# A streaming encoder layer on one core: the input projection by one level of Strassen's scheme

## The reference, cut to what matters

```
h  = rmsnorm(x, g1)
z  = h @ w_in                      # 1024 x 8200: mq mk mv mo | i f | sb sc sx | dq dk dv | gt (3 x 1024)
ya = sigmoid(mo) * rmsnorm(mlstm(mq, mk, mv, i, f))          # 4 heads, recurrence over 5 token chunks
yb = sb * dwconv3(sc * sx)
yc = rmsnorm(diff_attention(dq, dk, dv))                     # prompt (chunk mask) and sample (1024 cached keys)
x  = x + sum_b(sigmoid(gt_b) * (y_b @ w_branch[b])) @ w_out
h2 = rmsnorm(x, g2);  up = dwconv3(h2 @ w_up)                # 1024 x 5632
x  = x + (silu(up[:2816]) * up[2816:]) @ w_down;  y = rmsnorm(x)
```

## Time and profile before

| | |
|---|---|
| median of 3 runs | 1053.42 us (1052.29 to 1055.95) |
| the profiled execution | 1055.69 us, of which the span is 1053.9 us |
| mean granted TensorE clock | 0.986 of 2.4 GHz |
| PE busy | 97% of the span, 8074 matmuls |
| DVE, ACT, POOL busy | 49%, 33%, 17% |
| DMA | 92 MB, 88 GB/s on average |

### The profile page before, as it was taken

One profiled execution on the slowest core, in us unless ns is written; L12 is line 12 of the kernel. 1 busy time (PEld: TensorE's weight loads), 2 busy tenths in 40 slices (PEclk: granted clock), 3 DMA queues, 4 the chain that ended last, 5 costly groups with the idle time before them and its releaser, 6 DMA issues.

```text
span 1053.9 us, 19077 instructions
## 1 busy us (share of the span) xinstructions
PE 1020.5 (97%) x8074; PEld 994.4 (94%) x8074; DVE 519.3 (49%) x782; ACT 348.6 (33%) x616; POOL 180.1 (17%) x357
## 2 busy tenths in 40 slices
PE   5999999979999999999999999999999999999996
PEld 4899899978988999999999999999999999999996
DVE  6543243413344447234325444777777777533332
ACT  5333232423344333222223332333333433222221
POOL 4101223200222122300002120112211212110010
PEclk8999999989999999999999999999999999999998
DMA  6223214371112142131512422223322222332212
GB/s 186 81 81 85 76 51 123 94 224 56 41 41 81 41 121 81 49 99 55 151 49 71 131 81 81 80 81 96 105 81 81 80 81 84 104 94 86 83 56 86
DMA packets 93452, 92.46 MB, mean 88 GB/s; under 512 B 3492, under 2 KB 86329, under 8 KB 93367
## 3 DMA queue, kind: packets, MB, share of 16 engines
q1 hardware_dynamic: 88559, 82.09, 25.4%
q10 hardware_dynamic: 3784, 6.29, 2.0%
q0 software_dynamic: 1024, 2.86, 1.0%
HBM read 86.15 MB, written 5.08 MB: 87 GB/s over the span
## 4 chain that ended last, share of the span: by engine, by line
PE 92%; DVE 3%; DMA 2%; ACT 1%; POOL 1%; issue 0%; ACTq 0%; DVEq 0%
PE D L1319 83%; DMA ck<-in_cache_k 2%; PE X L1500 1%; PE X L1536 1%; DVE hn_x L1040 1%; PE D L1403 1%; PE X L1470 1%; PE X L1505 1%; PE X L1450 0%; PE X L1447 0%; PE X L1448 0%; PE X L1432 0%; DMA x_t<-in_x_prompt 0%; PE X L1519 0%; PE X L1486 0%
## 5 line engine op out<-in xcount | busy, mean ns | idle before, releaser
L1319 PE MATMUL D<-h_h,w_h 128*128 128x272 f32 (+1 forms) x1744 | 365.7, 291 | 6.8 <-DVE h_l L1034 5.0
L1319 PE MATMUL D<-h_h,w_l 128*128 128x272 f32 (+1 forms) x1744 | 362.0, 289 | 0.0
L1319 PE MATMUL D<-h_l,w_h 128*128 128x272 f32 (+1 forms) x1744 | 360.9, 289 | 0.0
L985 DVE TENSOR_TENSOR w_l<-raw,w_h 128x1024 fp32r<-128x1024 f32 (+3 forms) x172 | 196.8, 1145 | 192.9 <-ACT w_h L752 188.1
L1319 PEld LDWEIGHTS D<-h_h,w_h 128*128 128x128 f32 (+1 forms) x1744 | 273.8, 189 | 9.8 <-issue 4.0
L1319 PEld LDWEIGHTS D<-h_l,w_h 128*128 128x128 f32 (+1 forms) x1744 | 274.8, 189 | 0.4
L1319 PEld LDWEIGHTS D<-h_h,w_l 128*128 128x128 f32 (+1 forms) x1744 | 272.6, 189 | 0.4
L752 ACT ACTIVATE w_h<-raw 128x1024 fp32r<-128x1024 f32 (+3 forms) x172 | 162.1, 943 | 105.0 <-PE D L1319 76.8
L953 ACT ACTIVATE acc<-ups,fcw 128x546 f32<-128x546 f32 x44 | 33.1, 753 | 163.9 <-POOL ffn_last L698 163.9
L1319 PE MATMUL D<-g_h,w_h 128*128 128x272 f32 x352 | 73.4, 290 | 1.8 <-ACT w_h L752 1.8
L1319 PE MATMUL D<-g_l,w_h 128*128 128x272 f32 x352 | 72.7, 288 | 0.0
(11 more groups left out here) (317 smaller groups left out, 1109.7 us busy)
## 6 DMA issues: line engine op xcount, KB each, us to landing
raw<-in_w_in SPq DMA_DIRECT2D x32, 1024.0 KB, 5.7
raw<-in_w_up SPq DMA_DIRECT2D x22, 1024.0 KB, 5.0
raw<-in_w_down SPq DMA_DIRECT2D x16, 704.0 KB, 4.5
raw<-in_w_branch SPq DMA_DIRECT2D x6, 1024.0 KB, 5.0
raw<-in_w_out SPq DMA_DIRECT2D x4, 1024.0 KB, 5.1
x_t<-in_x_prompt SPq DMA_DIRECT2D x4, 512.0 KB, 5.7
ck<-in_cache_k ACTq DMA_DIRECT2D x1, 2048.0 KB, 16.0
cv<-in_cache_v ACTq DMA_DIRECT2D x1, 2048.0 KB, 24.3
```

What stands on the lines that cost most here:

```text
L985: v.tensor_tensor(lo, src, hi.bitcast(F32), ALU.subtract).then_inc(S["wl_ready"], 1)
L1319: last = t.matmul(banks(n)[0:w.shape[2], half, 0:HALF], w[:, k, :], x[:, kx, HALF * half:HALF * half + HALF], start=kx == 0 and i == 0, st ...
```

## The change

The 64 blocks of the input projection and its gates, and the narrow one, are made in 33 pairs (32 of two 128-column blocks, and `i` with `f`). A pair is a matrix product of two token halves (272 each), two k halves (4 slices each) and two column blocks, and is done by seven products `p` of 4 slices, three terms and one token half: 12 matmuls each, 84 for a pair, where 2 blocks had 96. The other matmuls of the kernel stay.

- **Left operands.** Seven arrays (A11, A12, A22 and the sums S1 to S4, each 4 slices by 272), high and low parts, are made once at the start by DVE (`scaled`, `sum_left`, `low_left`) and ACT (`high_left`), spread over the first products (`left` units).
- **Right operands.** Three quarters of the weights are used as they are; four sums T4 to T7 of quarters, 512 wide, are made for each pair by DVE (`make_t`). Each of the seven is split by ACT and DVE into high and low parts, 512 wide.
- **Output.** Products 1, 6, 7 and 4 accumulate one after another in one PSUM bank, and ACT copies the bank out after each, 272 wide. Product 2 has a bank, 5 and 3 share one; DVE adds them to what ACT stored (three additions, 272 wide, per pair). Product 6 waits for ACT's copy of 1, 7 for that of 6, 4 for that of 7, and 3 for DVE's addition of 5.
- **What follows a block** now works on stored data: tanh over both blocks of a pair (1088 wide), the convolution's multiply and `sb`'s; the low parts of `ya` and `yb` go from POOL to DVE (1088 wide).
- **Slots.** Split weights come in five slots of 512 for all products of the kernel, split four units ahead; raw weights in four slots of half the size. The transposes `tok` (two of four 128-column tiles and one `tokS` of the sample tiles, per pair) use PSUM bank 1 alone, which product 2 and half of each `pr` use too.
- **Order.** Written anew: the recurrence's stage 2 and the next stage 0 follow product 7 of a pair, stage 1 follows product 3; `rows` 0, 1 and 2 stand among the first pairs; a step of the prompt attention comes after every five units of work (a `p` counts one, a `pr` two), from the second pair of `gt0` on; `sc`, `sx` and `sb` follow branch 0 all together. `cv` is loaded after `ck` 1, no longer beside `ck`.
- **Residual.** The seven arrays take the room of `xT`, so the transposed x is written to DRAM (`x_spill`, 2.2 MB, an ACT-queue DMA) after the first norm and read back before the output projection.

```diff
+NRAW, NSPLIT = 4, 5
+AHEAD = NSPLIT - 1
...
+A11, A12, A22, S1, S2, S3, S4 = range(7)
+LEFT = {1: A11, 2: A12, 3: S4, 4: A22, 5: S1, 6: S2, 7: S3}
+T_SLOT = {5: 0, 6: 1, 7: 2, 4: 3}
+QUARTER = {1: (0, 0), 2: (1, 0), 3: (1, 1)}
+A_PART = {A22: 5, S1: 6, S2: 7, S4: 8, S3: 9}
+LOW_AT = {A11: 4, A12: 4, S2: 5, S1: 6, S3: 7, A22: 8, S4: 9}
...
+    pair_banks = {pairs[0]: (0, 1, 3), pairs[1]: (2, 4, 5), pairs[2]: (6, 7, 3)}
+    pair_banks.update((q, (2 * (i % 2), 1, 3)) for i, q in enumerate(pairs[3:]))
...
+    unit("left", 0)
+    q_if, q_k0, q_k1, q_q0 = pairs[:4]
+    prod(q_if, 1, 2)
+    unit("left", 1)
+    prod(q_k0, 1, 2)
+    unit("left", 2)
+    prod(q_k1, 1, 2)
+    unit("left", 3)
+    prod(q_if, 6, 5)
+    unit("left", 4)
+    prod(q_k0, 6)
+    prod(q_if, 7)
+    unit("left", 5)
+    prod(q_k0, 5, 7)
+    prod(q_if, 4, 3)
+    prod(q_k0, 4, 3)
     unit("lam")
...
+    for u, q in enumerate((("dk", 1), ("dv", 0), ("dq", 0), ("dv", 1))):
+        follow(q, 7, "ml", 2, u)
+        follow(q, 7, "ml", 0, u + 1)
+        follow(q, 3, "ml", 1, u + 1)
+    follow(("dq", 1), 7, "ml", 2, 4)
...
+    for i, q in enumerate(queue):
+        prev, nxt = pairs[i + 2], queue[i + 1] if i + 1 < len(queue) else None
+        gated = prev[0][:2] == "gt"
+        toks = [tok] if prev[0] in ("mk", "mv", "dk", "dv") else []
+        a, other = pair_banks[q][0], 2 - pair_banks[q][0]
+        started = (q, 1) in [x[1] for x in ORDER if x[0] == "p"]
+        if prev == ("gt0", 3):
+            posts(prev, 0)
+            project(prev, 0, (0, 1), (0, 1))
+            project(prev, 1, (2, 3), (0, 1))
+            gated = False
+        if not started:
+            put(q, 1)
+        if gated and not started:
+            put(q, 5)
+            put(q, 6)
+            posts(prev, 0)
+            put(q, 2)
+        elif prev == ("gt0", 3):
+            put(q, 6)
+            put(q, 2)
+            put(q, 5)
+        else:
+            put(q, 2)
+            posts(prev, 0)
+            put(q, 6)
+            put(q, 5)
+            posts(prev, 1)
+        for f in toks:
+            f(prev, 0)
+        put(q, 7)
+        if gated:
+            project(prev, 0, (min(other, 1), max(other, 1)), (0, 1) if other == 0 else (1, 0))
+        elif nxt and not (q[0][:2] == "gt" and q != ("gt0", 0) and q != ("gt1", 0)):
+            put(nxt, 1)
+        for f in toks:
+            f(prev, 1)
+        put(q, 4)
+        for f in toks:
+            f(prev, 2)
+        put(q, 3)
+        if gated:
+            project(prev, 1, (min(a, 1), max(a, 1)), (1, 0) if a == 0 else (0, 1))
+    last = pairs[-1]
+    posts(last, 0)
+    project(last, 0, (0, 1), (0, 1))
+    project(last, 1, (2, 3), (0, 1))
     for j in range(KD):
         add("wo", j)
     unit("norm", 1)
...
...
+            waits_of[n] += {6: [n_of(q, 1)], 7: [n_of(q, 6)], 4: [n_of(q, 7)], 3: [n_of(q, 5)]}.get(w, [])
+            if w in (1, 2, 5):
+                last_user[banks_of[n][0]] = n_of(q, {1: 4, 2: 2, 5: 3}[w])
...
+        u6 = u_of(q, 6) - AHEAD
+        for w, e in ((7, u6 - 2), (6, u6 - 1), (5, u_of(q, 5) - AHEAD - 1), (4, u_of(q, 4) - AHEAD - 1)):
+            T_MAKES.setdefault(-1 if q == q_if else e, []).append((q, w))
...
+        def chain_bank(pair, w):
+            i = pair_banks[pair][{2: 1, 5: 2, 3: 2}.get(w, 0)]
+            return bank(i)[0:H if pair == q_if else P, 0:HALF]
...
+            def make_t(q, w):
+                i = pair_no[q]
+                B11, B12, B21, B22 = (quarter(q, k, blk) for k in range(2) for blk in range(2))
+                x, y, op = {7: (B22, B12, ALU.subtract), 6: (t_view(q, 7), B11, ALU.add), 5: (B12, B11, ALU.subtract),
+                            4: (B21, t_view(q, 6), ALU.subtract)}[w]
+                for k in {7: (0, 1), 6: (0,), 5: (0,), 4: (1,)}[w]:
+                    wait_item(dve, (q, k))
+                if i >= 2:
+                    dve.wait_ge(S["wl_ready"], u_of(pairs[i - 1], w) + 1)
+                if w in (6, 4):
+                    dve.wait_ge(S["t_ready"], t_no[(q, {6: 7, 4: 6}[w])] + 1)
+                v.tensor_tensor(t_view(q, w), x, y, op).then_inc(S["t_ready"], 1)
...
+                            scaled(k, 1, f_21[:, k, :])
+                            scaled(k + KQ, 1, a_f[:, A22, k, :])
+                        dve.wait_ge(S["f_ready"], 16)
+                        sum_left(S1, f_21[:], a_f[:, A22], ALU.add)
+                        dve.wait_ge(S["s_ready"], 1)
+                        sum_left(S2, a_f[:, S1], f_half[:, 0], ALU.subtract)
+                    elif a[0] == 1:
+                        dve.wait_ge(S["s_ready"], 2)
+                        sum_left(S4, f_half[:, 1], a_f[:, S2], ALU.subtract)
+                        dve.wait_ge(S["s_ready"], 3)
+                        low_left(S2)
+                    elif a[0] == 2:
+                        low_left(S1)
+                        sum_left(S3, f_half[:, 0], f_21[:], ALU.subtract)
+                    else:
+                        low_left({3: S3, 4: A22, 5: S4}[a[0]])
                 elif kind == "norm":
...
+                    dve.wait_ge(S["dense_done"], n + 1)
+                    wait_drained(dve, n_of(q, {2: 1, 3: 6}.get(w, 7)))
+                    out, src = dst_of(q, *{2: (0, 0), 3: (1, 0)}.get(w, (1, 1))), chain_bank(q, w if w in (2, 3) else 5)
+                    v.scalar_tensor_tensor(out=out, in0=src, scalar=scale_of(q), in1=out, op0=ALU.mult, op1=ALU.add)\
+                        .then_inc(S["dve_drained"], 1)
...
+                elif kind == "left":
+                    if a[0] == 0:
+                        act.wait_ge(S["f_ready"], 16)
+                        act.dma_start(x_spill, xT0[:]).then_inc(S["x_out"], 16)
+                        high_left(A22, ("f_ready", 16))
+                        high_left(S1, ("s_ready", 1))
...
+                elif kind == "p" and a[1] in (1, 6, 7, 4):
+                    q, w = a
+                    blk, half = {1: (0, 0), 6: (1, 0), 7: (1, 1), 4: (0, 1)}[w]
...
+                    act.dma_start(xT[:], x_spill).then_inc(S["x_back"], 16)
...
+            def strassen_product(n, q, w):
+                g, left = first_unit[n], LEFT[w]
+                pe.wait_ge(S["wl_ready"], g + 1)
+                if q == q_if and w > 2:
+                    pe.wait_ge(S["al_ready"], LOW_AT[left])
+                wh, wl, out = split_view(w_h, g), split_view(w_l, g), chain_bank(q, w)
+                for k in range(KQ):
+                    if q == q_if and w == 1:
+                        pe.wait_ge(S["al_ready"], k + 1)
+                    for i, (wt, x) in enumerate(((wh, a_h), (wh, a_l), (wl, a_h))):
+                        last = t.matmul(out, wt[:, k, :], x[:, left, k, :], start=w in (1, 2, 5) and k == i == 0,
+                                        stop=k == KQ - 1 and i == 2, skip_group_check=True)
+                last.then_inc(S["dense_done"], 1)
...
+                        dve.wait_ge(S["x_back"], 16)
```

1048 lines of the change are left out of this document (601 added, 447 removed), and 3 rows, old and new, of the table ML_ORDER.

## The result

| | before | after |
|---|---|---|
| median of 4 runs | 1053.72 us (1052.29 to 1055.95) | 1107.80 us (1106.51 to 1108.14) |
| ratio | | 1.0509, 95% interval 1.0493 to 1.0524 |
| profiled execution, span | 1053.9 us | 1106.2 us |
| mean granted clock of the span | 0.986 | 0.964 |

The change makes the kernel 5.1% slower. 1062 us were predicted, with 1088 as the upper end: the sign was right, the size was not, and the range missed it by 20 us.

What follows compares the result with a forecast made beforehand. PE was taken to bound the kernel, DVE the `sc` to `sb` stretch. From 1055.7 us, -43.5 for matmuls and added waits sum to +8.5, 1064.2; the median of runs is 2.3 lower: 1062 us, range 1026 to 1088.

Steps and rivals of the forecast that it cites:

- the pauses at `rows`: Among the first pairs, DVE and ACT bursts outlast PE's cover: +12 us taken, bounds 5 and 15.
- `ck`: Load behind the recurrence: the 5.3 us wait grows by up to 1.5; with `sample` and `mo` +4 us, bounds 0 and 7.
- the start: Until PE is in full flow at about 57 us, making the left operands costs +7 us, bounds +4 and +12.
- `sc` to `sb` stretch: Six pairs after branch 0: DVE needs 99.0 us against PE's 81.5, so +19 us, bounds 10 and 24.
- A: Rival for the waits at `rows`, recurrence and `sample`: bursts are absorbed, faster, 1033 us; chance with its far end 0.27.
- D: Rival on the matmul count: the change doesn't save the matmuls, time above 1100 us; chance 0.01.
- B: Rival on DVE: every added instruction costs its full duration, +15 to 20 us, 1079 us; chance with beyond 0.18.
- -43.5 + the waits: Whole kernel: 348 fewer matmuls at 0.125 us save 43.5 us, and added waits are put against that: +8.5 us.
- the recurrence: Four recurrence steps: DVE's stage 1 makes PE wait 1.5 to 1.9 us each, +7 us, bounds 2 and 10.
- the attention beside branch 0: Gate pairs with attention steps: PE 21.3 us against DVE 19.2, PE stays the bound, +1 us, bounds 0 and 5.
- branch 2: Late stretch counted in the rest: DVE stays hidden, +1 us for the change-over, bounds 0 and 3.
- The upper bounds of the waits: All added waits at their largest, about 80 us together, give 1090 us.

Runs made afterwards that it cites:

- its best version: Changed kernel with attention only beside gates, tok transposes in banks 4 and 5, `rows` 1 cut, branch 2's product 2 first, transpose copies on ACT: 1082.76 us, ratio 1.0281.
- after_best: Changed kernel with attention, bank, `rows` 1, product 2 and transpose-copy edits, plus idle matmuls (24 and 48) in two pauses: 1082.44 us, ratio 1.0268.

## Why the prediction was wrong, step by step

**Right: what bounds, the matmuls, most of the waits.** 7726 matmuls; PE's pace of 0.125 at full clock; the pauses at `rows` (3.8, 4.6 and 4.6 us for 2.3, 5.4 and 4.7, the second released by the copy into `mk_tok` that the text named); `ck` 7.2 us for 5.3 + up to 1.5; the start, 4.4 for 7 with the lower bound at 4; 20.6 for 19 in the `sc` to `sb` stretch. That the three pauses at `rows` add up to the forecast is partly luck, since the first was 1.5 us longer and the second 0.8 shorter. No rival took place. The bursts were not absorbed (A). The matmuls were saved (D): its time, above 1100, came true, but the count is 7726 and the pace at full clock 0.125. B's 1079 was too low, and its reason fails too, as DVE's next instruction still starts 0.60 us after a split:

```profile
75.99 0.67 DVE L1226 TENSOR_TENSOR w_l<-tw,w_h 128x512 fp32r<-128x512 f32 x1
76.59 0.42 DVE L1379 SCALAR_TENSOR_TENSOR mkT<-D,mkT 128x272 f32<-128x272 f32 x1
```

**The step that failed: "-43.5 + the waits" as the whole sum.** It priced each wait at its length and took every matmul at 0.125 us. The sum lacked 44 us (1064.2 for 1108.0). 11 of them are waits that were longer or not foreseen (63.2 for 52); the other 32.6 are time in which the matmuls that are left ran slower: 19 us of granted clock, some 12 us at the edges of the interruptions. The clock stood in the text for the start's upper bound alone, although shows what a pause does in mid-kernel: 26 matmuls in six us behind the 5.3 us wait, where the earlier trace rows has 8 in each (though 16 of the 26 are transposes of 128 columns). By its pace a matmul is 0.10 us dearer there. The five long pauses that came (3.8, 4.6, 4.6, 7.2 and 5.45 us, three of them foreseen at about this length) have 6.8 us at the low level each, up to 3 us beyond themselves, and the eight other stretches of 3.4 us 1.5 each. The fills show that the clock is a real cost in this kernel (10.5 us from four pauses), and also that it doesn't always come back as time: two other fills gave nothing that can be told.

**Mis-sized: the recurrence, 10.0 for 7; the attention beside branch 0, 3.2 for 1.** Same mechanism as foreseen, longer chains.

**Missing: branch 2, 7.4 for 1.** The text asked whether PE has enough work beside DVE's and found that it had. It did not follow who frees the place that ACT's copy of product 1 needs. Before, a gate block was copied by a tanh of its own block, 9 us apart; now the copy stands between products 1 and 6.

**Right number, partly wrong reason: `sc` to `sb`.** The text had DVE busy for over 90% of the stretch. It was busy for 83.2 of 111 us, 75%, and PE idle for 16.9:

```profile
375.00:486.00 111.00, 94.11 (x661) 85.04 (x660) 83.16 (x162) 50.29 (x135) 22.53 (x52) 0.95 0.21 58
```

So it is no full engine that holds PE up, but in-order lists that wait for each other by turns: the longest wait, 5.45 us, is for ACT's `y_tmp`, and ACT itself had stood 8.0 us for a sum of DVE's that came behind a convolution:

```profile
438.46 0.79 DVE L1538 SCALAR_TENSOR_TENSOR scb<-u_c,vec,scb 128x546 f32<-128x546 f32 x1
...
439.89 0.68 DVE L1241 TENSOR_TENSOR tw<-tw,raw 128x512 f32<-128x512 f32 x1
...
440.61 0.63 ACT L985 ACTIVATE w_h<-tw 128x512 fp32r<-128x512 f32 x1 [8.02 <-DVE tw L1241]
...
443.50 0.36 ACT L1188 ACTIVATE y_tmp<-X,vec 128x128 f32<-128x128 f32 x1
...
444.01 1.09 PE L1849 MATMUL X<-ident,prob 128*128 128x128 f32 x4 [5.45 <-ACT y_tmp L1188]
```

Taking work from DVE helps (11.6 and 34 us), but a comparison of sums, 99.0 against 81.5, gave the right cost by luck as much as by method.

**The range.** The upper bounds of the waits (about 80 us) gave 1090, and the range ended at 1088. A cost that multiplies the waits belonged to it. By what was measured here it is 0.5 us of slower matmuls for each us of added pause (32.6 by 63.2), which on 80 us is 40 and would have moved the upper end to 1130; the clock alone (0.3) would have moved it to about 1114.

## What to carry to other kernels

A matmul saved on a PE that never waits is worth its pace only if nothing else begins to wait: here 43.5 us of matmuls were paid with 63 us of waits, and the waits with some 19 us of clock and 12 at their edges. When a forecast creates pauses on PE, price the long ones with the slow matmuls that follow one in the profile at hand, not with their length alone. Where such a pause can't be avoided, matmuls that nobody reads can hold the clock; whether the time follows has to be measured: it did in one of three kernels here. And in-order engines that wait for each other lose time long before one of them is full, so cut a burst and look at what stands behind it before comparing sums of busy time.

## What the runs showed of the hardware

- Eight pauses of PE in a dense stretch, in one execution: those of 0.3 to 1.92 us left the granted clock at full; those of 2.35, 2.64 and 2.93 us were each followed by 3.4 us at 1.2 GHz. In other traces pauses of 1.6 to 1.9 us were sometimes followed by such a stretch and pauses of 2.25 to 2.65 us sometimes not (44 of 70 of 2 to 3 us were). The five longest of the changed kernel (3.8 to 7.2 us) had 6.8 us each. A matmul of 272 columns then starts every 0.227 us, not every 0.125.
- Idle matmuls in the pauses kept the clock at 1.00 each time. Four of them gave 10.5 us in the changed kernel; two in its best version and one in the kernel before gave nothing that can be told from the spread.
- At full clock an interruption of PE costs more than the profile's idle time: 0.16 us hidden under the last record, and often some 0.1 us more before the second matmul behind it.
- Sums of 128x512 on POOL took 1.5 us, and DVE's splits took 0.90 us in the mean for 0.72, the longest 4.0: moving two-input work from DVE to POOL gave nothing.
- The spread between runs of a kernel goes in part with the mean granted clock: in `after_best` spans of 1072.9 us at 0.984 and 1084.1 at 0.972, but in the version with attention beside gates 1093.6 at 0.968 and 1095.0 at 0.960.
